# Attention and projection of a decoder step: queries copied earlier in the program, other slots and steps, value columns added by GpSimd

## The reference, cut to what matters

```
h = rmsnorm(x, norm1_g)
b_c, c_c, h_c, q, k, v, f_logit, q_m = split(h @ w_in)       # 2568 columns
mk, mv = split(rmsnorm(mem_prompt) @ w_mem_kv)
logf = log_sigmoid(f_logit + b_f)
y_conv = b_c * causal_conv3(c_c * h_c)
y_fox  = softmax(mask(q k^T/8 + cumsum(logf)_q - cumsum(logf)_k)) v   # 8 heads of 64
y_mem  = softmax(q_m mk^T/8) mv                                     # 4 heads of 64
x = x + concat(norm(y_conv), norm(y_fox), norm(y_mem)) * g @ w_out
x = x + (silu(h2 @ w_gate) * (h2 @ w_up)) @ w_down;  y = rmsnorm(x)
```

## Time and profile before

| | us |
|---|---|
| median of 3 runs | 2776.25 (2769.03 to 2781.96) |
| profiled execution | 2769.61, span 2767.9, granted clock 0.98 |
| projection | 0 to 543.7 |
| attention | 543.7 to 1154 |
| combination; gate and up; down | 1154 to 1390; to 2313; to the end |

### The profile page before, as it was taken

How to read it: one execution, slowest core, us unless ns; L and a number is a source line. 1 busy time by engine, 2 the same in 40 slices (tenths; PEclk the granted TensorE clock), 3 DMA queues, 4 the chain that set the end, 5 groups by cost and what they waited for, 6 DMA issues and landing times. The chain is left out here.

```text
span 2767.9 us, 42326 instructions
## 1 busy us (share of the span) xinstructions
PE 2632.1 (95%) x14745; PEld 2377.2 (86%) x14745; DVE 1935.7 (70%) x2560; ACT 1169.0 (42%) x2012; POOL 1694.4 (61%) x963
## 2 busy tenths in 40 slices
PE   8999989889999998899979999999989999999998
PEld 7999889877777777677879999999989997887887
DVE  5366696478888887676577778878787875445664
ACT  4212321367777777633343333333433332223343
POOL 3486678488999998655556675666666660222232
PEclk9999999989999999999989999999999999999999
DMA  6588789566666677776635433543434546754564
GB/s 210 167 266 253 252 268 319 170 178 169 176 176 172 176 185 194 214 251 197 203 78 182 133 112 115 168 130 113 130 112 129 172 118 191 243 178 168 185 221 141
DMA packets 471365, 499.21 MB, mean 180 GB/s; under 512 B 172123, under 2 KB 359446, under 8 KB 470122
## 3 DMA queue, kind: packets, MB, share of 16 engines
q1 hardware_dynamic: 449730, 469.97, 56.3%
q10 hardware_dynamic: 21136, 25.50, 2.7%
q0 software_dynamic: 288, 1.05, 0.1%
HBM read 398.07 MB, written 94.16 MB: 178 GB/s over the span
## 5 line engine op out<-in xcount | busy, mean ns | idle before, releaser
L2613 PE MATMUL ps_gate_up<-h_hi,w_hi 128*128 128x344 f32 (+1 forms) x1848 | 593.7, 321 | 26.2 <-DVE h_lo L2503 14.2
L2615 PE MATMUL ps_gate_up<-h_hi,w_lo 128*128 128x344 f32 (+1 forms) x1848 | 594.0, 321 | 0.0
L2614 PE MATMUL ps_gate_up<-h_lo,w_hi 128*128 128x344 f32 (+1 forms) x1848 | 593.4, 321 | 0.0
L2613 PEld LDWEIGHTS ps_gate_up<-h_hi,w_hi 128*128 128x128 f32 x1848 | 349.9, 189 | 29.7 <-DVE h_lo L2503 16.4
L2614 PEld LDWEIGHTS ps_gate_up<-h_lo,w_hi 128*128 128x128 f32 x1848 | 350.2, 190 | 0.0
L2615 PEld LDWEIGHTS ps_gate_up<-h_hi,w_lo 128*128 128x128 f32 x1848 | 350.1, 189 | 0.0
L878 PE MATMUL ps_proj<-w_hi,h_hi 128*128 128x428 f32 (+1 forms) x800 | 289.3, 362 | 10.0 <-ACT proj_out L602 9.9
L879 PE MATMUL ps_proj<-w_lo,h_hi 128*128 128x428 f32 (+1 forms) x800 | 285.4, 357 | 0.0
L880 PE MATMUL ps_proj<-w_hi,h_lo 128*128 128x428 f32 (+1 forms) x800 | 284.9, 356 | 0.0
L1595 DVE TENSOR_TENSOR p_lo<-ps_turned,p_hi 128x512 fp32r<-128x512 f32 (+1 forms) x352 | 211.0, 614 | 81.5 <-ACT p_hi L1483 80.0
L2390 POOL TENSOR_TENSOR stock<-common 128x512 f32<-128x512 f32 x65 | 104.2, 1602 | 251.0 <-DVE w_lo L2488 235.9
(11 more groups left out here) (346 smaller groups left out, 6574.3 us busy)
## 6 DMA issues: line engine op xcount, KB each, us to landing
stock<-in_cache_k SPq DMA_DIRECT2D x192, 256.0 KB, 3.4
common<-in_cache_v SPq DMA_DIRECT2D x172, 256.0 KB, 3.1
stock<-act_combined SPq DMA_DIRECT2D x56, 704.0 KB, 4.2
common<-in_w_gate SPq DMA_DIRECT2D x33, 1024.0 KB, 5.3
common<-in_w_up SPq DMA_DIRECT2D x33, 1024.0 KB
common<-in_w_down SPq DMA_DIRECT2D x44, 512.0 KB, 5.8
page_v<-in_cache_v SPq DMA_DIRECT2D x84, 256.0 KB, 3.1
common<-in_w_in SPq DMA_DIRECT2D x44, 428.0 KB, 4.9
```

Of the source, the lines that this page charges most:

```text
L2613: pe.matmul(acc, a_hi, h_hi[:, m, d, 0:n], start=d == 0, stop=False)
L2614: pe.matmul(acc, a_hi, h_lo[:, m, d, 0:n], start=False, stop=False)
L2615: mm = pe.matmul(acc, a_lo, h_hi[:, m, d, 0:n], start=False, stop=d == H - 1)
```

## The change

It has four parts.

1. Projection: the own keys' block moves from step 64 to 76 (its load from 61 to 73), the memory tiles' squares from 58 to 68 and their normalisation from 62 to 71, the sample gate's chain on ACT from 47 to 50 and its last operation on DVE from 48 to 51.
2. Attention, tables: other slots for turns, pieces and the values' split, and a table of its own for the 15 slots before head 0.
3. The copy of a Turn's queries is issued in the Turn's own slot, behind the queries' high part and ahead of the next unit's `p_hi`.
4. GpSimd adds the two halves of a running value sum after each eighth group; PE then takes one half instead of two.

```diff
-    GATES_AT, OWN_AT, CUM_AT = 58, 64, 6
+    GATES_AT, OWN_AT, CUM_AT = 58, 76, 6
...
-            load_step[u], square_step[u], normal_step[u] = 54, 58, 62
+            load_step[u], square_step[u], normal_step[u] = 54, 68, 71
...
-                    if n == 47:
+                    if n == 50:
                         act.wait_ge(s.gs_x, 1)
...
-                    if n == 48:
+                    if n == 51:
                         dve.wait_ge(s.gs_low, 1)
...
-FIRST_AT = (0, 1, 3, 3, 5, 5, 6, 7, 7)
+FIRST_AT = (0, 1, 3, 3, 5, 5, 6, 6, 7)
 SECOND_AT = (0, 1, 2, 3, 4, 5, 7, 7)
-THIRD_AT = (0, 1, 3, 3, 4, 4, 5, 6, 8, 9, 10, 12)
-MEMORY_LEAD_AT = (0, 1, 2, 4, 5, 7, 8, 9, 11, 11)
-MEMORY_AT = (0, 0, 2, 2, 3, 4, 4, 6, 6, 8)
+THIRD_AT = (0, 1, 3, 3, 3, 4, 5, 7, 8, 8, 10, 14)
+START_AT = (1, 1, 2, 4, 4, 4, 6, 7, 8, 9, 10, 11)
+MEMORY_LEAD_AT = (0, 1, 2, 4, 4, 5, 7, 8, 11, 13)
+MEMORY_AT = (0, 0, 1, 2, 3, 3, 4, 5, 6, 8)
...
-        return ([Turn(head, "kq", 0), Turn(head, "kq", 1)] + fox_pieces(head, range(3)) + [SplitV(head)] + fox_pieces(head, range(3, 6)) +
-                [Turn(head, "kq", 2)] + fox_pieces(head, range(6, 8)))
+        return ([Turn(head, "kq", 0), Turn(head, "kq", 1)] + fox_pieces(head, range(2)) + [SplitV(head)] +
+                fox_pieces(head, range(2, 5)) + [Turn(head, "kq", 2)] + fox_pieces(head, range(5, 8)))
...
+                    if g % PGROUPS == PGROUPS - 1:
+                        both = a.page_sum[:, b % 2]
+                        pool.wait_ge(s.added, g + 1)
+                        pool.tensor_tensor(both[:, 0], both[:, 0], both[:, 1], ALU.add).then_inc(s.row_summed, 1)
...
-                        pe.wait_ge(s.added, PGROUPS * (b + 1))
+                        pe.wait_ge(s.row_summed, b + 1)
                         out = bank(("row", b))
-                        for e in range(2):
-                            mm = pe.matmul(out[0:1, :], c.ones[:], a.page_sum[:, b % 2, e, :], start=(e == 0), stop=(e == 1))
-                        mm.then_inc(s.row_made, 1)
+                        pe.matmul(out[0:1, :], c.ones[:], a.page_sum[:, b % 2, 0, :], start=True, stop=True).then_inc(s.row_made, 1)
...
-                    for item in items_at(n - 1):
-                        if isinstance(item, Turn) and item.side == "kq":
-                            cols = slice(item.j * BLK, (item.j + 1) * BLK)
-                            act.wait_ge(s.in_hi, turn_index[item] + 1)
-                            act.dma_start(a.q_hi[0:HD, cols].bitcast(F32), a.q_hi[HD:P, cols].bitcast(F32)).then_inc(q_copied[item.j], 16)
...
                                 act.activation(a.q_hi[HD:P, cols], src[HD:P], ACT.Copy, scale=SCALE).then_inc(s.in_hi, 1)
+                                act.wait_ge(s.in_hi, turn_index[item] + 1)
+                                act.dma_start(a.q_hi[0:HD, cols].bitcast(F32), a.q_hi[HD:P, cols].bitcast(F32)).then_inc(q_copied[item.j], 16)
```

More of the change, by code:

```diff
@@ L952, in fox_pieces @@
     return out
-FIRST_AT = (0, 1, 3, 3, 5, 5, 6, 7, 7)
+FIRST_AT = (0, 1, 3, 3, 5, 5, 6, 6, 7)
 SECOND_AT = (0, 1, 2, 3, 4, 5, 7, 7)
-THIRD_AT = (0, 1, 3, 3, 4, 4, 5, 6, 8, 9, 10, 12)
-MEMORY_LEAD_AT = (0, 1, 2, 4, 5, 7, 8, 9, 11, 11)
-MEMORY_AT = (0, 0, 2, 2, 3, 4, 4, 6, 6, 8)
+THIRD_AT = (0, 1, 3, 3, 3, 4, 5, 7, 8, 8, 10, 14)
+START_AT = (1, 1, 2, 4, 4, 4, 6, 7, 8, 9, 10, 11)
+MEMORY_LEAD_AT = (0, 1, 2, 4, 4, 5, 7, 8, 11, 13)
+MEMORY_AT = (0, 0, 1, 2, 3, 3, 4, 5, 6, 8)
 def lead_items(head):
     if is_fox(head):
-        return ([Turn(head, "kq", 0), Turn(head, "kq", 1)] + fox_pieces(head, range(3)) + [SplitV(head)] + fox_pieces(head, range(3, 6)) +
-                [Turn(head, "kq", 2)] + fox_pieces(head, range(6, 8)))
+        return ([Turn(head, "kq", 0), Turn(head, "kq", 1)] + fox_pieces(head, range(2)) + [SplitV(head)] +
+                fox_pieces(head, range(2, 5)) + [Turn(head, "kq", 2)] + fox_pieces(head, range(5, 8)))
     pieces = [Piece(head, tuple(range(QCH * ch, QCH * ch + QCH)), 0, MEM, True) for ch in range(NT // QCH)]
-    return [Turn(head, "k", 0), Turn(head, "q", 0), Turn(head, "q", 1), pieces[0], SplitV(head), pieces[1], Turn(head, "q", 2), Turn(head, "q", 3), pieces[2], pieces[3]]
+    return [Turn(head, "k", 0), Turn(head, "q", 0), Turn(head, "q", 2), Turn(head, "q", 1), pieces[0], SplitV(head), pieces[1], Turn(head, "q", 3), pieces[2], pieces[3]]
 def memory_items(head):
@@ L974, in memory_items, with first_items @@
     return [Turn(head, "k", 0), Turn(head, "q", 0), Turn(head, "q", 1), pieces[0], SplitV(head), Turn(head, "q", 2), pieces[1], Turn(head, "q", 3), pieces[2], pieces[3]]
+def first_items():
+    return [Turn(0, "kq", 0), Turn(0, "kq", 1)] + fox_pieces(0, range(2)) + [SplitV(0)] + fox_pieces(0, range(2, 6)) + [Turn(0, "kq", 2)] + fox_pieces(0, range(6, 8))
 def at_slots(slots, items):
@@ L985, in attention_phases @@
     heads = FH + MH
-    phases = [([], list(enumerate(lead_items(0))))]
+    phases = [([], at_slots(START_AT, first_items()))]
     for h in range(heads):
@@ L1015, in attend @@
     for own, work in attention_phases():
-        span = len(own) or len(work) + 3
+        span = len(own) or max(at for at, _ in work) + 4
         phase_start.append((slot, len(units)))
@@ L1130, in attend @@
         ps_o = psum("ps_out", [P, BLK])
-        names = ("low_zeroed in_turned q_copied0 q_copied1 q_copied2 q_copied3 k_hi in_hi in_lo turned t_hi t_lo pv scored min made probs v_hi v_lo o_copied o_ready inverted o_out row_made row_out "
+        names = ("row_summed low_zeroed in_turned q_copied0 q_copied1 q_copied2 q_copied3 k_hi in_hi in_lo turned t_hi t_lo pv scored min made probs v_hi v_lo o_copied o_ready inverted o_out row_made row_out "
                  "q0 q1 k0 k1 v0 v1 decay page0 page1 page2 weighed halved added st0 st1 st2 st3 row_st0 row_st1 "
```

## The result

The changed kernel takes 2754.45 us (median of 5 runs, 2751.15 to 2763.06) against 2774.24 before (5 runs, 2768.44 to 2781.96): a ratio of 0.9944, 95% interval 0.9923 to 0.9966. A second series of the same program, beside other runs, gave 0.9938 (0.9911 to 0.9964). The prediction was 2758.6 us, 0.994. The time is right; several of the parts it was added up from are not, and most of what follows is on that.

A forecast was written before the change was run, and what follows sets the result against it. PE bounds the kernel, so edits gain from its work or gaps: 2.0 + 7.1 + 5.5 + 3.0 = 17.6 us off the median 2776.25 gives 2758.6 us (0.994), bounds some 8 us either side.

The forecast's parts named there:

- sample gate: Projection, step 47 to 50: PE's 2.95 us wait for ACT's evacuation shrinks to about 1; 2.0 us gained, ends 0 and 4.3.
- memory tiles with own keys: Projection: moved DVE blocks let SP load sooner, shrinking the evacuation wait; 7.1 of 9.8 us lost gained, bounds 2 and 9.8.
- GpSimd adds the halves: Attention: PE does half the matmuls of eight value sums, GpSimd's 10 us hidden; 5.5 us gained, bounds 3 and 7.2.
- turns in memory heads: Attention, odd slots: waits for queries' low parts go, the keys' 3.3 us stay; 3.0 us gained, ends 0 and 6.7.
- the other slots: Attention, values' split, third-phase pieces, lead before head 0: PE's work the same, first piece as late; 0, ends -3 and +3.
- the copy's issue: Attention, ACT: the copy can't start sooner, 0 gained; issuing 32 times ahead of `p_hi` taken as 0, ends 0 and +15.
- the moved work fills places where DVE waits for GpSimd: Projection, steps 71 and 76: cover for the moved blocks; without it, 9.5 us of the same delay later.
- rival B: Projection: the delay only moves, about 7 us of wait at step 76 or 80; 10.5 off, 2765.8 us; chance 0.20.
- this costs nothing on PE unless pages come late: Attention: GpSimd's adds hidden, PE taking sums 18 slots later; without cover up to 2 us per late sum, 10 in all.
- The rival in which more goes right: Step 71's wait goes whole, copy waits halve, slow clocks go too: 15 us more, 2743.6 us; chance 0.10.
- the first sign: Projection's end: the forecast would be wrong if the projection ends later than 538 us.

The follow-up runs named there:

- the hold on the page loads: Changed kernel, with SP holding back the value page group due around a head's first two turns until the second copy of queries landed: 0.9923, median 2748.42 us.
- the first pieces later: Changed kernel, with the first two pieces of a head one slot later (slot 4), the next two at 5 and 6: 0.9949.

## Why the prediction was right, and where it was not

The sum, 17.6 us, is what was measured (15.5 to 17.2 by the two ratios). Its terms, one by one, in us:

| step of the prediction | forecast | measured |
|---|---|---|
| sample gate, and memory tiles with own keys | 2.0 + 7.1 | 7.2 together, alone (3.6 to 10.8) |
| GpSimd adds the halves | 5.5, hidden | 2.8 alone, 1 to 3 within the change |
| turns in memory heads | 3.0 | 2.7 of waits gone |
| the other slots | 0 | about 9 alone (11.9 for all tables, 8.3 to 15.5), less beside the rest |
| the copy's issue | 0 | 0.3 |

*Sample gate.* Right: the wait went from 2.95 to 1.12 us.

*Memory tiles and own keys.* The chain from DVE over SP and ACT to PE was right, and step 71 is regular now. The step "the moved work fills places where DVE waits for GpSimd" was too good: the chain formed again eight steps later, so in the profiled execution 9.1 us were saved there (5.3 + 4.8 instead of 19.2) and 10.2 + 6.6 - 9.4 = 7.4 lost. The prediction had this as its rival B, but as all or nothing; it stood at 5 us or more in four of the eight profiles with these steps and this pace, those in which DVE starts its scores behind GpSimd's product.

*The adds.* The matmuls, the adds' time and their place in GpSimd's waits were all as said. Missed was that the other terms shorten attention and take away the cover of GpSimd's end: "this costs nothing on PE unless pages come late" should have been checked at the stage's end, with attention already 10 us shorter. The adds gave some 2 us back at the hand-over. Missed too was that the third phases get longer with them, by 2 to 7 us: that cost was put at nothing, and in the profile of the adds alone it takes the whole saving.

*The other slots.* "0, ends -3 and +3" was the largest miss, in the favourable direction. Its reason, that the first piece behind the copy is as late as before, held; but the waits for `p_lo` fell from 8.9 to 5.7 us, and PE's busy time by 3.5. That the table spreads the work on DVE is the likely reason and is not shown. With the adds and the projection overrated by some 5 us together and this term underrated by 9, the rest is what the parts do to each other (attention's parts are worth 15.0 us singly and 7.8 together): the right total is partly luck.

*The copy's issue.* Right in both halves: it can't start sooner, and of the 15 us upper end 4 showed as waits for `p_lo` and none in the time, as far as its interval tells (3.9 faster to 3.6 slower). The rival in which more goes right held that the new slots would shrink the copy's waits; they hardly did (14.5 us of waits of scores without a releaser or for the copy, after 15.3), but the hold on the page loads did what it asked for, and with it went the slow clock behind each wait, as that rival had it.

*The signs of being wrong.* The prediction named two, a projection that ends later than 538 us and an attention over 605 us. Measured as it was before, to attention's first matmul, the projection ends at 538.9 us instead of 543.7, so the first sign stands, by 0.9 us and because of the wait at step 80. Attention takes some 603 us by the same marks and stays below. The forecast of the projection, 9.1 us, was too high, as its 7.2 (3.6 to 10.8) says too.

## What to carry to other kernels

For a small transfer on the critical path (here 128 KB within SBUF), look at which bulk loads are in flight when it is issued, and try letting the queue of the bulk loads wait for it. Here that took 10 us off the third phases in the profile and gave the lowest ratio (0.9923 against 0.9938 and 0.9944, with overlapping intervals), where an earlier place in the issuing engine's program gave 0.9999. Count with a wait the slow clock behind it, which here was the larger part. When several edits shorten a stage, ask again for each what hid under the old length, above all the work of the slowest other engine at the stage's end. And a delay that comes from one engine's overload moves with the work that is moved: count the load at the new place before booking the old wait as gain, and look at who starts first where two engines hold each other up: here a start 0.03 us ahead or behind went with a wait under 2 us or over 5.

## What was not expected of the hardware

The same copy of 128 KB within SBUF takes 2.2 us from issue to landing by itself and up to 6.1 us beside 256 KB page loads of another queue (the first pieces later, head 5). An operation of DVE on 128x256 took 0.43 us when it started 0.04 us ahead of a product of GpSimd, and 4.5 us when it started 0.4 us behind one. An activation that stands behind a DMA's issue on ACT started 0.57 us after the issue's start (599.98 to 600.55), while an issue that stood behind the activation started together with it. And two medians of the same changed program, of 5 and of 12 runs, lay 5 us apart (2754.45 and 2759.76), as much as most terms here: only ratios to runs of before beside them tell such terms apart, and 2 us not even they.
